# Cross attention, log gates and key positions in products of halves: one kernel on one core

## The reference, cut to what matters

```
# gated linear attention, log gates: rank 16 per direction, W2 is 16 x 256
la_fw = log_sigmoid(lr_fw @ w2[0] + gb[0]) / 16 ;  la_bw = log_sigmoid(lr_bw @ w2[1] + gb[1]) / 16

# latent attention (layer 1): 32 rotary key columns out of h @ w_dq_dkv
cq, ckv, k_pe = split(h @ w_dq_dkv, [384, 640]) ;  k_pe = apply_rope(k_pe, cos, sin)

# cross attention, once per layer: 4 heads of 256, 512 tokens, 256 memory rows
q = h @ wq ;  k, v = split(m @ wkv, 2)
s = einsum("bthd,bmhd->bhtm", q, k) * 256 ** -0.5
o = einsum("bhtm,bmhd->bthd", softmax(s), v) ;  out = o @ wo
```

## Time and profile before

| | |
|---|---|
| runs | 2039.12, 2043.26, 2039.18 us |
| the profiled execution | 2043.49 us in all, 2041.7 us from first to last instruction |
| TensorE matmul / weight loads | 2010.7 us (98%) / 1623.9 us (80%) |
| VectorE, ScalarE, GpSimd | 918.8, 592.2, 1437.2 us |
| granted TensorE clock, mean | 0.995 |
| cross attention, layer 0 and 1 | 905.97 to 937.51 and 1592.79 to 1624.33 us |

### The profile page before, as it was taken

The page is one execution under the profiler, slowest core; times in us unless marked ns, Lnnn a source line. Parts: engine busy times, 40 slices in busy tenths (PEclk is TensorE's granted clock), DMA queues, the critical chain, the costliest instruction groups (busy, mean ns, idle before and its releaser), DMA issues.

```text
span 2041.7 us, 25336 instructions
## 1 busy us (share of the span) xinstructions
PE 2010.7 (98%) x9348; PEld 1623.9 (80%) x9348; DVE 918.8 (45%) x1531; ACT 592.2 (29%) x1115; POOL 1437.2 (70%) x732
## 2 busy tenths in 40 slices
PE   8999989999999999999999999999999999999997
PEld 6787778888888888787888888877678788888886
DVE  4556544243444897524431422444643454223143
ACT  5455442221114344413210110226731321111011
POOL 7523379777877878864877778787568288777773
PEclk9999999999999999999999999999999999999998
DMA  4742233233223354221333323223013123333221
GB/s 162 140 56 70 74 109 107 99 95 100 97 85 111 104 156 159 97 93 42 95 101 93 101 89 99 82 91 114 1 45 100 42 85 107 98 94 103 93 88 57
DMA packets 57049, 190.64 MB, mean 93 GB/s; under 512 B 6256, under 2 KB 8048, under 8 KB 56848
## 3 DMA queue, kind: packets, MB, share of 16 engines
q1 hardware_dynamic: 52752, 182.58, 29.6%
q10 hardware_dynamic: 4192, 6.58, 1.0%
HBM read 183.37 MB, written 2.10 MB: 91 GB/s over the span
## 4 chain that ended last, share of the span: by engine, by line
PE 97%; DVE 1%; ACT 1%; DMA 0%; POOL 0%; issue 0%; SPq 0%; DVEq 0%; ACTq 0%
PE bank L694 29%; PE bank L696 29%; PE bank L695 29%; PE bank L1340 2%; PE bank L1110 1%; PE bank L1027 1%; PE bank L1370 1%; PE bank L939 1%; PE bank L1354 1%; PE bank L1089 1%; PE bank L754 0%; PE bank L1049 0%; PE bank L1100 0%; DMA raw<-weights 0%; PE bank L883 0%; DVE MIX L2764 0%
## 5 line engine op out<-in xcount | busy, mean ns | idle before, releaser
L603 POOL TENSOR_TENSOR wH<-raw,zero 128x1024 fp32r<-128x1024 f32 (+1 forms) x304 | 573.2, 1886 | 416.6 <-PE bank L696 398.7
L606 POOL TENSOR_TENSOR wL<-raw,wH 128x1024 fp32r<-128x1024 f32 (+1 forms) x304 | 718.6, 2364 | 23.9
L694 PE MATMUL bank<-hnH,wH 128*128 128x512 f32 (+1 forms) x1464 | 578.7, 395 | 13.9 <-POOL wL L597 7.5
L695 PE MATMUL bank<-hnL,wH 128*128 128x512 f32 (+1 forms) x1464 | 572.3, 391 | 0.0
L696 PE MATMUL bank<-hnH,wL 128*128 128x512 f32 (+1 forms) x1464 | 572.2, 391 | 0.0
L694 PEld LDWEIGHTS bank<-hnH,wH 128*128 128x128 f32 (+1 forms) x1464 | 274.8, 188 | 80.8 <-DVE hnL L2059 15.2
L695 PEld LDWEIGHTS bank<-hnL,wH 128*128 128x128 f32 (+1 forms) x1464 | 275.0, 188 | 59.7 <-issue 2.4
L696 PEld LDWEIGHTS bank<-hnH,wL 128*128 128x128 f32 (+1 forms) x1464 | 274.8, 188 | 59.6 <-issue 0.9
L694 PE MATMUL bank<-actH,wH 128*128 128x512 f32 x784 | 307.0, 392 | 0.0
L696 PE MATMUL bank<-actH,wL 128*128 128x512 f32 x784 | 305.1, 389 | 0.0
L695 PE MATMUL bank<-actL,wH 128*128 128x512 f32 x752 | 292.6, 389 | 0.0
(11 more groups left out here) (367 smaller groups left out, 2448.8 us busy)
## 6 DMA issues: line engine op xcount, KB each, us to landing
raw<-weights SPq DMA_DIRECT2D x315, 512.0 KB, 3.5
raw<-weights SPq DMA_DIRECT2D x28, 384.0 KB, 3.0
XT<-x_t SPq DMA_DIRECT2D x8, 256.0 KB, 6.3
XT<-x_t ACTq DMA_DIRECT2D x1, 2048.0 KB, 9.2
out<-MIX ACTq DMA_DIRECT2D x8, 256.0 KB, 2.2
maxB<-rowM SPq DMA_DIRECT2D x7, 256.0 KB, 14.2
qkO<-qkA SPq DMA_DIRECT2D x4, 256.0 KB, 4.1
memT<-mem_t ACTq DMA_DIRECT2D x1, 1024.0 KB, 5.3
```

The lines of the kernel that those rows point to most:

```text
L603: nc.gpsimd.tensor_tensor(wH[:, slot, 0:w], raw[:, slot, 0:w], nothing.broadcast_to([P, w]), ALU.add)\
L606: nc.gpsimd.tensor_tensor(wL[:, slot, 0:w], raw[:, slot, 0:w], wH[:, slot, 0:w].bitcast(F32), ALU.subtract).then_inc(split, 1)
L694: mm(out_, aH, bH, start=first, stop=False)
L695: mm(out_, aH, bL, start=False, stop=False)
```

## The change

**Cross attention.** Queries, keys, probabilities and values are split into halves, and scores and values use `three` (three single-pass products for one full-precision product). Each query tile is now scaled in PSUM by VectorE, copied to a high half by ScalarE, and its low half is subtracted by VectorE, which frees the tile. The memory's high halves are made by ScalarE in eight copies behind the inverse root; VectorE subtracts the eight low halves (from SBUF, in place), one beside each query, the last behind the last query. The turned probabilities are copied to a high half by ScalarE; the low half is subtracted by VectorE, which now frees the tile, in its queue behind the inverse sums of the next head. The negated maxima move from VectorE to ScalarE.

**Log gates.** W2 is loaded three times into 96 rows; rows 0 to 31 and 64 to 95 hold its high half, 32 to 63 its low half; the ranks are stacked as high, high, low. One single-pass product over 96 rows takes the place of a full-precision one over 32.

**Key positions.** GpSimd writes the high and low half of the 128 x 32 weights side by side. A product with 64 columns of weights against the high half of the input gives both at once, a product with 32 against the low half gives the third: 16 products. The low part lies in rows 32 to 63; it is turned with the rest, and VectorE adds it behind the turn, ahead of the rotation.

```diff
...
@@ -562,7 +567,8 @@
                         sp.dma_start(CT[:, :], consts).then_inc(tables_in, 16)
-                        sp.dma_start(W2[:, :, :], gla_w2).then_inc(tables_in, 16)
+                        for part in range(3):
+                            sp.dma_start(W2[32 * part:32 * part + 32, :, :], gla_w2).then_inc(tables_in, 16)
                     if u0 + i0 == RING - 1:
@@ -605,6 +611,17 @@
                                         ALU.subtract).then_inc(split, 1)
+
+            def split_stacked(u, slot, turn):
+
+                pool.wait_ge(loaded[slot], turn * 16 + 16)
+                src = raw[:, slot, 0:KD * 32].rearrange("p (k c) -> p k c", k=KD)
+                both = wH[:, slot, 0:KD * 64].rearrange("p (k c) -> p k c", k=KD)
+                nc.gpsimd.tensor_tensor(both[:, :, 0:32], src, nothing.unsqueeze(1).broadcast_to([P, KD, 32]), ALU.add)\
+                    .then_inc(hi_split, 1)
+                pool.wait_ge(hi_split, u - skipped[0] + 1)
+                nc.gpsimd.tensor_tensor(both[:, :, 32:64], src, both[:, :, 0:32].bitcast(F32), ALU.subtract)\
+                    .then_inc(split, 1)
@@ -943,9 +962,10 @@
                 n = TILE0["log_a"] + i
-                gone_wait(pe, TILE0["lr_gates"])
+                pe.wait_ge(sig("ranks_high"), 3)
+                pe.wait_ge(sig("ranks_low"), 1)
                 claim(n)
-                mm(psum(n)[:, :], W2[:, i // 2, (i % 2) * P:(i % 2) * P + P], lrT[:, :], start=True, stop=True)\
+                mm(psum(n)[:, :], W2S[:, i // 2, (i % 2) * P:(i % 2) * P + P], lrS[:, :], start=True, stop=True)\
                     .then_inc(tile_done, 1)
@@ -1083,11 +1103,13 @@
                         gone_wait(pe, TILE0[f"xq{l}"] + 2 * h + 1)
+                        pe.wait_ge(sig("x_memory_low"), 8 * l + h + 1)
                         for q in range(2):
                             for k in range(2):
-                                last = mm(psum(n)[:, q * MEM:q * MEM + MEM], qX[:, 2 * h + k, tok],
-                                          KT[l][:, 2 * h + k, :], start=(k == 0), stop=(k == 1))
+                                last = three(psum(n)[:, q * MEM:q * MEM + MEM], qH[:, 2 * h + k, tok],
+                                             actL[:, 2 * h + k, tok], actH[:, 2 * h, k * MEM:k * MEM + MEM],
+                                             KL[l][:, 2 * h + k, :], k == 0, k == 1)
                         last.then_inc(tile_done, 1)
                     gone_wait(pe, xtile(base, "t", h, 1))
+                    pe.wait_ge(sig("x_memory_low"), 8 * l + 4 + h + 1)
                     for f in range(2):
                         for m in range(2):
-                            last = mm(psum(n)[:, :], VM[l][:, m, h * 256 + f * P:h * 256 + f * P + P],
-                                      PX[:, h % 2, m, :], start=(m == 0), stop=(m == 1))
+                            at_ = m * 256 + f * P
+                            last = three(psum(n)[:, :], actH[:, 2 * h + 1, at_:at_ + P],
+                                         VL2[l][:, m, h * 256 + f * P:h * 256 + f * P + P],
+                                         PXH[:, h % 2, m, :], PXL[:, h % 2, m, :], m == 0, m == 1)
                         last.then_inc(tile_done, 1)
@@ -1224,11 +1249,14 @@
                     claim(n)
-                cut = slice(k * 32, k * 32 + 32)
-                last = three(psum(n)[0:32, :], wH[:, u % RING, cut], wL[:, u % RING, cut], hnH[:, k, :], hnL[:, k, :],
-                             k == 0, k == KD - 1)
-                if k == KD - 1:
-                    last.then_inc(unit_done, 1)
+                both = (psum(n)[0:64, :], wH[:, u % RING, k * 64:k * 64 + 64], hnH[:, k, :])
+                high = (psum(n)[0:32, :], wH[:, u % RING, k * 64:k * 64 + 32], hnL[:, k, :])
+                if k < KD - 1:
+                    mm(*both, start=k == 0, stop=False)
+                    mm(*high, start=False, stop=False)
+                else:
+                    mm(*high, start=False, stop=False)
+                    mm(*both, start=False, stop=True).then_inc(unit_done, 1)
@@ -1525,6 +1553,10 @@
                      scale=-1.0), n)
+            gone_wait(act, TILE0["lr_gates"])
+            run(W2S[:, :, :], W2[:, :, :], ACT.Copy).then_inc(sig("ranks_high"), 1)
+            for part in range(2):
+                run(lrS[32 * part:32 * part + 32, :], lrT[:, :], ACT.Copy).then_inc(sig("ranks_high"), 1)
@@ -1853,6 +1885,15 @@
                 row_root(TILE0[f"row_sum_x{l}"])
+                for h in range(4):
+                    run(actH[:, 2 * h, :].rearrange("p (k m) -> p k m", k=2), KT[l][:, 2 * h:2 * h + 2, :], ACT.Copy)\
+                        .then_inc(sig("x_memory_hi"), 1)
+                for h in range(4):
+                    run(actH[:, 2 * h + 1, :].rearrange("p (m e) -> p m e", m=2), VM[l][:, :, h * 256:h * 256 + 256],
+                        ACT.Copy).then_inc(sig("x_memory_hi"), 1)
+                for i in range(KD):
+                    act.wait_ge(sig("x_q_scaled"), KD * l + i + 1)
+                    run(qH[:, i, :], psum(TILE0[f"xq{l}"] + i)[:, :], ACT.Copy).then_inc(sig("x_q_hi"), 1)
@@ -1860,8 +1901,8 @@
                             tile_wait(act, xtile(base, "o", h - 2, 1))
-                        free(run(PX[:, h % 2, :, pair * MEM:pair * MEM + MEM],
-                                 psum(n)[:, :].rearrange("p (m q) -> p m q", m=2), ACT.Copy), n)
+                        run(PXH[:, h % 2, :, pair * MEM:pair * MEM + MEM],
+                            psum(n)[:, :].rearrange("p (m q) -> p m q", m=2), ACT.Copy).then_inc(sig("x_rows"), 1)
@@ -1874,6 +1915,7 @@
                             tile_wait(act, xtile(base, "t", h - 1, pair))
+                        link(run(xst[:, pair, 2:4], xst[:, pair, 0:2], ACT.Copy, scale=-1.0 / 16))
                         for q in range(2):
@@ -2248,6 +2290,9 @@
                 .then_inc(sig("rows_ready"), 1)
+            dve.wait_ge(sig("ranks_high"), 2)
+            tt(W2S[32:64, :, :], W2[32:64, :, :], W2S[32:64, :, :].bitcast(F32), ALU.subtract)
+            tt(lrS[64:96, :], lrT[:, :], lrS[0:32, :].bitcast(F32), ALU.subtract).then_inc(sig("ranks_low"), 1)
@@ -2581,8 +2626,38 @@
                 root_wait()
+
+                def query_low(i):
+                    n = TILE0[f"xq{l}"] + i
+                    dve.wait_ge(sig("x_q_hi"), KD * l + i + 1)
+                    free(tt(actL[:, i, :], psum(n)[:, :], qH[:, i, :].bitcast(F32), ALU.subtract), n)
+
+                def memory_part(i):
+                    dve.wait_ge(sig("x_memory_hi"), 8 * l + i + 1)
+                    h = i % 4
+                    if i < 4:
+                        dst, src = (t[:, 2 * h:2 * h + 2, :] for t in (KL[l], KT[l]))
+                        hi = actH[:, 2 * h, :].rearrange("p (k m) -> p k m", k=2)
+                    else:
+                        dst, src = (t[:, :, h * 256:h * 256 + 256] for t in (VL2[l], VM[l]))
+                        hi = actH[:, 2 * h + 1, :].rearrange("p (m e) -> p m e", m=2)
+                    tt(dst, src, hi.bitcast(F32), ALU.subtract).then_inc(sig("x_memory_low"), 1)
                 for i in range(KD):
-                    scaled(qX[:, i, :], TILE0[f"xq{l}"] + i)
+                    n = TILE0[f"xq{l}"] + i
+                    tile_wait(dve, n)
+                    tt(psum(n)[:, :], psum(n)[:, :], rstd[:, :], ALU.mult).then_inc(sig("x_q_scaled"), 1)
+                    if i < KD - 1:
+                        memory_part(i)
+                    query_low(i)
+                memory_part(KD - 1)
+
+                def rows_low(h):
+                    for pair in range(2):
+                        n = xtile(base, "t", h, pair)
+                        dve.wait_ge(sig("x_rows"), 8 * l + 2 * h + pair + 1)
+                        own = (slice(None), h % 2, slice(None), slice(pair * MEM, pair * MEM + MEM))
+                        free(tt(PXL[own], psum(n)[:, :].rearrange("p (m q) -> p m q", m=2), PXH[own].bitcast(F32),
+                                ALU.subtract), n)
@@ -2594,17 +2669,19 @@
                         tile_wait(dve, n)
-                        link(nc.vector.reduce_max(xst[:, pair, 0:2], psum(n)[:, :].rearrange("p (q m) -> p q m", q=2),
-                                                  AX.X))
-                        ts(xst[:, pair, 2:4], xst[:, pair, 0:2], -1.0 / 16, None, ALU.mult).then_inc(sig("x_max"), 1)
+                        nc.vector.reduce_max(xst[:, pair, 0:2], psum(n)[:, :].rearrange("p (q m) -> p q m", q=2),
+                                             AX.X).then_inc(sig("x_max"), 1)
                     for pair in range(2):
                         last.then_inc(sig("x_probs"), 1)
+                    if h >= 1:
+                        rows_low(h - 1)
                     if h >= 2:
                         output_low(h - 2)
+                rows_low(3)
                 output_low(2)
@@ -2689,8 +2766,13 @@
             dve.wait_ge(sig("turned"), 4)
```

(9 more changed lines are left out.)

29 lines of the change are left out of this document (18 added, 11 removed).

## The result

| | before | after |
|---|---|---|
| median of the runs | 2039.24 us (5 runs, 2039.12 to 2043.26) | 2029.33 us (5 runs, 2029.21 to 2031.04) |
| ratio, 95% interval | | 0.9941 [0.9931, 0.9952] |
| profiled execution, its span | 2043.49, 2041.7 us | 2029.21, 2027.3 us |
| cross attention, layer 0, from the first score product to the second product behind it | 31.61 us | 29.03 us |

The account below looks back on a forecast made before the run. TensorE, busy for 98% of the span and 97% of the chain, was taken as the bound. Log gates 3.2, key positions 1.8 and cross attention 2.8 summed to 7.8 us off: 2031.4 us against the median, range 2026.5 to 2038.

Parts of the forecast that it names:

- Log gates, 3.2: Four gates, each two instructions of 1.05 us made one single-pass product of 0.23: 3.2 us off TensorE.
- The cover: Before the first decay: ScalarE's 8.07 us idle ahead of the values was to hide added copies' delay of 2.2 to 4.
- Key positions, 1.8: Key position projection: 24 products become 16, taken as 1.8 us off TensorE.
- The port, "in time": Cross attention's last memory part requests SBUF 0.05 to 0.13 us before GpSimd's next operation starts and gets in.
- the alternative: Last memory part loses the port to GpSimd, walk ends 0.93 us later than before per layer: 2036.1 us, chance 0.27.
- The new wait: Cross attention: TensorE stalls for VectorE's low rows, queued behind the next head's probabilities, 0.9 to 1.0 us twice per layer.
- the walk: Cross attention's queues priced step by step: values 3 end at 30.12 us; old queues give 31.22 for the measured 31.54.
- its 1.4: Cross attention's gain per layer, 31.54 - 30.12 us, after stalls behind VectorE; 2.8 us for two layers.
- 4.3 net: Cross attention, TensorE alone per layer: 5.1 us saved by halves, less 0.2 at up to four transpose-to-halves switches.
- 3 of the 4.3 come back: Cross attention: of TensorE's 4.3 us gain per layer, 3 return as stalls behind VectorE.
- A: The forecast case: low rows stall TensorE, last memory part gets in; 2031.4 us, alone 2029.5 to 2034, chance 0.55.
- Rival C: Cross attention without stalls, queues overlapping better than walked: 13.6 us off, 2025.6 us, chance 0.11.

Follow-up runs that it names:

- 6: Changed kernel with six tiny one-column VectorE copies ahead of the last memory part of each cross attention: 2033.78 us, ratio 0.9964.
- 8: Changed kernel without low halves of the turned rows; value products take the high halves twice, so the result is incomplete: 2027.23 us, ratio 0.9933.
- 12: Changed kernel with last memory part one query earlier, low-row products last, head 0's output halves between head 3's maxima and probabilities, head 1's later: 2026.10 us, ratio 0.9927.
- 10: Changed kernel with the two low-row products of each value tile put last, TensorE waiting for low rows only then: 2029.82 us, ratio 0.9943.
- 7: Changed kernel with the last memory part subtracted one query earlier: 2029.77 us, ratio 0.9942.
- 9: Changed kernel with ScalarE's row copies ahead of the next exponentials and VectorE's low rows ahead of the next head's probabilities: 2029.48 us, ratio 0.9943.
- 5: Changed kernel with two tiny one-column VectorE copies ahead of the last memory part of each cross attention: 2029.41 us, ratio 0.9943.
- 4: Kernel before with only the log gates changed to one single-pass product each: 2037.79 us, ratio 0.9985.
- 3: Kernel before with only cross attention changed to halves, gates and key positions as before: 2035.24 us, ratio 0.9971.
- experiment 1: Kernel before, run and profiled again without an edit: 2041.33 us, ratio 1.0.
- 2: Kernel before with the log gates and key positions changed, cross attention as before: 2034.76 us, ratio 0.9970.
- the early part and low rows last: Changed kernel with the last memory part one query earlier and each value tile's low-row products last: 2026.60 us, ratio 0.9929.

## Why the prediction was right, and where it wasn't

- **Log gates, 3.2:** 3.6 measured, alone and with the rest. The cost of a first single-pass product behind full-precision work, which the forecast let cancel, isn't paid at two of the four gates (they gain 1.0 and not 0.8). The cover was used up to its upper estimate (4.1 us) and held.
- **Key positions, 1.8:** 1.9.
- **The port, "in time":** right. The request came 0.14 us ahead of GpSimd's start, just above the forecast's 0.05 to 0.13, and 6 shows that the alternative was real: VectorE's operation took 2.72 us, and each stretch 2.4 more. The forecast gave it 0.27.
- **The new wait:** right in kind and place. TensorE waits for low rows of heads 0 and 2 and for probabilities of heads 0 and 3, by name what the walk had; 8 shows that without low rows the wait goes.
- **Its size is the term that failed.** The walk had stalls of 0.73, 0.96, 0.28, 0.77, 0.96 and 0.09, in all 3.79; measured are 0.69, 0.77, 0, 0.45, 0.66 and 0, in all 2.57. The two waits for low rows were to be 0.9 to 1.0. The walk charged 0.70 for a low half and 0.72 for a maximum, the length of one from the earlier trace rows; back to back their starts are 0.60 apart (903.51 to 904.11, and two low rows in 1.20, 911.87 to 913.07), since an instruction's end overlaps the next one's start. The walk worked out again by its own rules, with 0.60 for these two and nothing else changed, ends 1.36 us sooner, at 28.8 (an estimate). Measured are 28.80 instead of 30.12, so this one price explains the difference. No run changes the price alone.
- **Two ends mixed.** The forecast took its 1.4 from the measured 31.54, the end of the last value product, and the walk's 30.12, which like 28.80 is without that product's last 0.16 us. Like with like it was 31.38 - 30.12 = 1.26. So the measured 2.58 is 1.32 more than the walk gives, and 1.16 more than the forecast.
- **TensorE alone, "4.3 net":** too small. The halves save 5.1 by their products, and with no stall (12) 5.1 are measured: 31.61 - 26.51. The 0.8 for going from transposes back to halves isn't there on top. The walk has 0.2 of it at two places (scores of head 2 end at 10.44, where its prices add up to 10.25; values 1 at 21.73 instead of 21.53), and without its stalls gives 30.12 - 3.79 = 26.33. That is near the measured 26.28, so the 4.3 didn't reach the sum. "3 of the 4.3 come back" isn't what the walk adds up to either: it saves some 5 and gives back 3.8. (An estimate by four passes for true FP32, the Trainium skill, FP8 and Floating Point Precision, TensorE Precision Notes, is 6.9; the traces stay at the rows' 5.1.)
- **A reading:** 7.07 us for 32 score instructions would be 0.221 each. The 0.216 of the text is right all the same: the product behind them starts at 912.87, 6.90 after the first.
- **The sum:** 3.6 + 1.9 + 2 x 2.6 = 10.7 by the products' places, 9.9 by the medians, 7.8 forecast. The measured 2029.33 is inside the whole range, but 0.2 us under the 2029.5 that the text gave as the lower end of A alone: the mechanism was A's, stronger than A was priced. Rival C, no stalls at all, was the time of another program: 2025.6 was its price, and the kernel of 12 takes 2026.10.
- The forecast named a stretch under 28.5 or over 31.5 as what would refute it; 28.80 is inside, by 0.3, and TensorE didn't wait ahead of the first weights of head 0.

## What to carry to other kernels

When another engine begins to pace a stretch, price its steps by the distance of two starts and not by the length of one; here 0.60 against 0.70 was the error. A stall behind an operand that only some products need goes away by doing the others first, and a wait of the pacing engine is where its deferrable work belongs. With the last memory part moved to where there is cover, these moves (10, 7 and 12) took 28.80 to 26.28 us without removing an instruction, while one that only moved the wait (9) gave nothing. Measure a stretch between the same kind of points before and after: here two ends that looked alike differed by 0.16 us. Where an operation's price hangs on its request coming ahead of another engine's, move it to where there is cover (7).

## What the runs showed of the hardware

- The request order between VectorE's operation with two SBUF inputs and GpSimd's decides within some hundredths of a microsecond: 0.01 us ahead VectorE's operation took 0.68 us (5), 0.03 behind 2.92, 0.22 behind 2.72 (6). Where it waits, VectorE's operation ends 0.54 us after GpSimd's.
- Profiles of nearly equal kernels differ in places where the granted clock differs. Its rise after the start: the first product of short distance starts at 10.9 us in one profile (4) and at 17.3 in another (3). A fall for some microseconds between 1485 and 1505 us costs 1.7 us in four of the fourteen profiles (before, 4, 9, 12); TensorE idled twice, for 1.09 and 1.05 us, ahead of it in the profile of before, but for 1.06 and 1.05 at the same place in that of experiment 1, which has no fall. The last row sums cost 0.95 more in four (before, 2, 3, 10). The program of before has only two profiles, which differ in the last two. Together the three make up to about 4.7 us, nearly the spread of its runs (2038.90 to 2043.95 in the later sets).
- A fourth place is behind an idle time of TensorE of 5.57 us: the product at 282.25 in the profile of the changed kernel (282.23 with the early part and low rows last) starts at the lower level, and how long it stays there varies. Windows of 284 to 288, the changed kernel and then that one, in which the same products behind come 1.4 us sooner:

```profile
284.00:288.00 4.00, 4.00 (x11) 3.03 (x11) 3.83 (x6) 3.29 (x6) 1.65 (x2) 0.50 0.02 9
```

```profile
284.00:288.00 4.00, 4.00 (x16) 3.20 (x16) 3.82 (x6) 3.29 (x6) 1.64 (x2) 0.86 0.01 5
```
